# Paged attention whose every second sample reads latents stored turned

## The reference, cut to what matters

```python
past_c = cache_latent[j][page_table].reshape(bs, past_len, KV_LORA)      # 8 x 4096 x 256
past_r = cache_krope[j][page_table].reshape(bs, past_len, ROPE_DIM)      # 8 x 4096 x 64
past_k = cache_kscale[j][page_table].reshape(bs, past_len, MLA_HEADS)    # 8 x 4096 x 8
s = (jnp.einsum('bqhr,bkr->bhqk', ql, c) + jnp.einsum('bqhp,bkp->bhqk', qr, kr))
s = s * ks * SOFTMAX_SCALE
p = jax.nn.softmax(s, axis=-1)
o = jnp.einsum('bhqk,bkr->bqhr', p, c)
```

## Time and profile before

| | us |
|---|---|
| median of 3 runs | 3991.21 (3987.98 to 3994.84) |
| time of the profiled execution | 3988.52 |
| its span | 3986.4 |
| first gather of `mla_dec` starts | 2234.61 |
| last `back` of `mla_dec` starts | 2446.85 |
| issue of the first load of the stage behind it | 2465.32 |

### The profile page before, as it was taken

One profiled execution on the slowest core, in us unless ns is written; L12 is line 12 of the kernel. 1 busy time (PEld: TensorE's weight loads), 2 busy tenths in 40 slices (PEclk: granted clock), 3 DMA queues, 4 the chain that ended last, 5 costly groups with the idle time before them and its releaser, 6 DMA issues. The chain is left out here.

```text
span 3986.4 us, 45941 instructions
## 1 busy us (share of the span) xinstructions
PE 3005.8 (75%) x14557; PEld 1439.4 (36%) x14557; DVE 2474.6 (62%) x6084; ACT 1535.0 (39%) x4402; POOL 1289.7 (32%) x1172
## 2 busy tenths in 40 slices
PE   7997888777666677768757798776777876666666
PEld 6886775322212122223313575322232222222221
DVE  2665443676676667767773343476677677667675
ACT  2352121444343344446432221344544444334332
POOL 0004330444434333333441110233334344334433
PEclk9998788988778788888878898888888988787778
DMA  2211002999999999999996453799999999999998
GB/s 89 73 51 55 13 13 71 404 420 416 420 414 418 405 397 387 411 366 384 402 421 244 165 204 144 291 375 390 381 375 415 405 404 421 413 420 413 411 421 334
DMA packets 234350, 1261.33 MB, mean 316 GB/s; under 512 B 32008, under 2 KB 71952, under 8 KB 97552
## 3 DMA queue, kind: packets, MB, share of 16 engines
q0 software_dynamic: 153600, 1133.58, 69.8%
q1 hardware_dynamic: 80528, 125.08, 9.1%
HBM read 1244.25 MB, written 14.19 MB: 316 GB/s over the span
## 5 line engine op out<-in xcount | busy, mean ns | idle before, releaser
L1951 PE MATMUL acc<-ring,diag 128*64 128x512 f32 x4096 | 1339.0, 751 | 751.3 <-ACT diag L1650 748.9
L1569 POOL DMA_INDIRECT ring<-in_uv,idx x1024 | 1119.1, 1093 | 1895.3 <-PE acc L1951 1635.2
L1761 DVE SCALAR_TENSOR_TENSOR ring<-ring,rep 128x1024 f32<-128x1024 f32 x1024 | 1230.6, 1221 | 368.9 <-DMA ring<-in_uv,idx 309.3
L1951 PEld LDWEIGHTS acc<-ring,diag 128*64 128x64 f32 x4096 | 250.3, 158 | 1494.2 <-ACT diag L1650 1317.8
L1642 ACT ACTIVATE hg<-hs 128x1 f32<-128x1 f32 x1024 | 203.7, 199 | 1141.1 <-DVE ring L1761 1139.1
L1650 ACT ACTIVATE diag<-const,hgg 128x64 f32<-128x64 f32 x1024 | 356.4, 348 | 33.4
L1646 ACT ACTIVATE hgg<-hg,weigh_by 128x1 f32<-128x1 f32 x1024 | 302.0, 295 | 33.2
L1883 PE MATMUL big<-xnT,w 128*128 128x264 f32 (+1 forms) x960 | 297.1, 435 | 0.0
L1883 PEld LDWEIGHTS big<-xnT,w 128*128 128x128 f32 x960 | 174.8, 203 | 185.0 <-issue 166.4
L298 PE MATMUL acc<-xnT,w 128*128 128x260 f32 x1024 | 230.2, 386 | 0.7 <-ACT inp L419 0.7
L298 PEld LDWEIGHTS acc<-xnT,w 128*128 128x128 f32 x1024 | 196.3, 192 | 38.4 <-issue 7.5
(11 more groups left out here) (571 smaller groups left out, 4057.7 us busy)
## 6 DMA issues: line engine op xcount, KB each, us to landing
w<-in_w_peer SPq DMA_DIRECT2D x64, 512.0 KB
w<-in_w_gdn SPq DMA_DIRECT2D x32, 512.0 KB, 3.6
ring<-in_uv,idx POOLq DMA_INDIRECT x1024, 12.3
wo<-in_w_mla_out SPq DMA_DIRECT2D x8, 1024.0 KB, 11.5
wo<-in_w_uq SPq DMA_DIRECT2D x8, 768.0 KB, 14.2
out_ssm_s<-states SPq DMA_DIRECT2D x4, 1024.0 KB, 5.1
wo<-in_w_gdn_out SPq DMA_DIRECT2D x4, 1024.0 KB, 8.2
sk<-in_keys SPq DMA_DIRECT2D x64, 64.0 KB
```

The lines of the kernel that those rows point to most:

```text
L1569: pool.indirect_dma_start(out=ring[:, c % RING, :], out_offset=None, in_=uv, in_offset=bass.IndirectOffsetOnAxis(ap=idx[u % 2][:, c:c + 1] ...
L1761: dve.scalar_tensor_tensor(ring[:, c % RING, 0:D], ring[:, c % RING, 0:D], 1.0, rep[:, 2 * a + c // RING, :], ALU.mult, ALU.mult, accum_ou ...
L1951: last = pe.matmul(acc[i][rows(j), :], diag[:, r, :], ring[:, r, D + HALF * j:D + HALF * j + HALF], start=r == 0, stop=r == RING - 1)
```

## The change

Samples with `a` = 0 stay as they were. For samples with `a` = 1 a second copy of the cache, `cache_turned`, prepared on the host, holds each page with the channels as rows: 128 rows of 320 numbers (128 positions of channels 0 to 127, the same of channels 128 to 255, and the rotary channels of two positions one above the other). GpSimd gathers it page by page, 32 DMAs of 128 rows each, into the one buffer `turned`, and the scores of these samples read `turned` directly, in runs of 4 numbers with a distance of 320 between runs. Their `flips` and the three copies behind them are gone. The latents of these samples are still gathered in the old layout too, since `values` needs them; their `keys` gather is gone. `mla_qkv` also makes `pages.row`, the 256 row-number columns for the page gathers. GpSimd's loop is written out.

```diff
@@ mla_qkv
+                sp.dma_start(pages.lane[:, :], core.i["lane"]).then_inc(s["page"], 16)
+                sp.dma_start(pages.all[:, :], core.i["page_table"].rearrange("(o b) g -> o (b g)", o=1).to_broadcast([P, NS * PAGES])).then_inc(s["page"], 16)
...
-                dve.wait_ge(s["page"], 80)
+                dve.wait_ge(s["page"], 112)
+                dve.tensor_copy(pages.rowf[:, :], pages.all[:, :]).then_inc(s["gains"], 1)
+                dve.scalar_tensor_tensor(pages.rowf[:, :], pages.rowf[:, :], float(PAGE), pages.lane[:, 0:1].to_broadcast([P, NS * PAGES]), ALU.mult, ALU.add).then_inc(s["gains"], 1)
+                dve.tensor_copy(pages.row[:, :], pages.rowf[:, :])
@@ mla_dec, GpSimd
+                def pages_turned(v):
+                    for g in range(PAGES):
+                        pool.indirect_dma_start(out=turned[:, g, :], out_offset=None, in_=core.i["cache_turned"],
+                                                in_offset=bass.IndirectOffsetOnAxis(ap=pages.row[:, PAGES * v + g:PAGES * v + g + 1], axis=0)).then_inc(s["lt1"], 16)
...
-                for a in range(2):
-                    keys(a)
-                    latents(a)
-                    factors(a)
-                with pool.Fori(1, TURNS) as i:
-                    for a in range(2):
-                        apart(pool, at("idx", i - 1, a + 1), at("flip", i - 1, NG * (a + 1)))
-                        keys(a)
-                        apart(pool, at(f"soft{a}", i - 1, 1))
-                        factors(a)
-                        apart(pool, at("pv", i - 1, a + 1))
-                        latents(a)
+                keys()
+                latents(0)
+                factors(0)
+                pages_turned(1)
+                latents(1)
+                factors(1)
+                for i in range(1, TURNS):
+                    after(pool, at("idx", i - 1, 1), at("flip", i - 1, NG))
+                    keys()
+                    after(pool, at("soft0", i - 1, 1))
+                    factors(0)
+                    after(pool, at("pv", i - 1, 1))
+                    latents(0)
+                    after(pool, at("idx", i - 1, 2), at("dotted", i - 1, 2 * NG))
+                    pages_turned(2 * i + 1)
+                    after(pool, at("soft1", i - 1, 1))
+                    factors(1)
+                    after(pool, at("pv", i - 1, 2))
+                    latents(1)
@@ mla_dec, TensorE
+                def latent(a, g, e, j):
+                    if a == 0:
+                        return cT[g % 2][:, e, j, :]
+                    first = PAGE * e + GRP * (BQ * g + j)
+                    return turned[:, :, first:first + GRP]
...
-                    if n or not first:
-                        after(pe, at("half0", i, n - 1), at("half1", i, n - 1))
-                    flips(i, a, g)
+                    if a == 0:
+                        if g == 0:
+                            after(pe, (s["lc0"], i * 16 + 16), (s["lr0"], i * 16 + 16))
+                        if g == NG // 2:
+                            after(pe, (s["ld0"], i * 16 + 16))
+                        if g or not first:
+                            after(pe, at("half0", i, g - 1), at("half1", i, g - 1))
+                        flips(i, g)
                     if n or not first:
-                        after(pe, at("half0", i, n), at("half1", i, n), at("keyr", i, n), at("lined", i, n - 1))
+                        if a == 0 and g:
+                            after(pe, at("half0", i, g), at("half1", i, g), at("keyr", i, g))
+                        if a and g == 0:
+                            after(pe, at("half0", i, NG), at("half1", i, NG), at("keyr", i, NG))
+                        if a and g == 1:
+                            after(pe, at("lt1", i, 16 * PAGES))
+                        after(pe, at("lined", i, n - 1))
```

More of the change, by code:

```diff
@@ L2135, in mla_qkv @@
     with Marks(core, "qkv", gains=1, q_made=1, q_out=1, k_made=1, k_square=2, q_square=1, rope=4, stat=11,
-               root=2, q_done=2, page=80, wuk=16, number=2) as s, ExitStack() as ctx:
+               root=2, q_done=2, page=112, wuk=16, number=2) as s, ExitStack() as ctx:
         sq = core.sbuf(ctx, "sq", [P, H, QK])
@@ L2252, in __init__ @@
         self.idx = [core.sbuf(ctx, "idx", [P, 1], U32) for _ in range(2)]
+        self.all = core.sbuf(ctx, "all", [P, NS * PAGES], mybir.dt.int32)
+        self.lane = core.sbuf(ctx, "lane", [P, 1])
+        self.rowf = core.sbuf(ctx, "rowf", [P, NS * PAGES])
+        self.row = core.sbuf(ctx, "row", [P, NS * PAGES], U32)
 def mla_dec(core, q, ckvT, krTs, ksc, wuv, os, pages):
@@ L2275, in mla_dec @@
         c = [core.sbuf(ctx, "c", [P, PER, KL]) for _ in range(2)]
-        kr = [core.sbuf(ctx, "kr", [P, PER, RD]) for _ in range(2)]
+        kr = core.sbuf(ctx, "kr", [P, PER, RD])
+        turned = core.sbuf(ctx, "turned", [P, PAGES, TURNED])
         ks = [core.sbuf(ctx, "ks", [P, PER, H]) for _ in range(2)]
@@ L2396, in _, with flips, rope @@
                 pe.matmul(pO[:, :], core.ident, core.const[:, C_ID:C_ID + 2, :].rearrange("p a c -> p (a c)"), start=True, stop=True)
-                def flips(i, a, g):
+                def flips(i, g):
                     for j in range(BQ):
[L2401 to L2404, removed]
+                        pe.transpose(b0[g % 2][:, j, :], c[0][:, BQ * g + j, 0:P], core.ident)
+                        pe.transpose(b1[g % 2][:, j, :], c[0][:, BQ * g + j, P:], core.ident)
+                    if g or not isinstance(i, int):
+                        after(pe, at("keyr", i, g))
                     for j in range(BQ // 2):
-                        last = pe.transpose(b2[:, j, :], kr[a][:, BQ * g + 2 * j:BQ * g + 2 * j + 2, :].rearrange("p j r -> p (j r)"), core.ident)
+                        last = pe.transpose(b2[:, j, :], kr[:, BQ * g + 2 * j:BQ * g + 2 * j + 2, :].rearrange("p j r -> p (j r)"), core.ident)
                     last.then_inc(s["flip"], 1)
+                def latent(a, g, e, j):
[3 more added lines that the diff above has]
+                    return turned[:, :, first:first + GRP]
+                def rope(a, g, j):
+                    if a == 0:
+                        return rT[g % 2][:, j // 2, :]
+                    first = 2 * PAGE + GRP * ((BQ * g + j) // 2)
+                    return turned[:, :, first:first + GRP]
                 def scores(a, g):
@@ L2412, in scores @@
                         for j in range(BQ):
-                            pe.matmul(pL[COLS * j:COLS * j + COLS, :], ql[a][:, e, :], cT[g % 2][:, e, j, :], start=e == 0, stop=False)
+                            pe.matmul(pL[COLS * j:COLS * j + COLS, :], ql[a][:, e, :], latent(a, g, e, j), start=e == 0, stop=False)
                     for j in range(BQ):
-                        last = pe.matmul(pL[COLS * j:COLS * j + COLS, :], qr[a][:, j % 2, :], rT[g % 2][:, j // 2, :], start=False, stop=True)
+                        last = pe.matmul(pL[COLS * j:COLS * j + COLS, :], qr[a][:, j % 2, :], rope(a, g, j), start=False, stop=True)
                     last.then_inc(s["dotted"], 1)
@@ L2455, in values @@
                     after(pe, at("exped", i, 2 * a + 2), at("v_out", i, a))
+                    if a:
+                        after(pe, (s["lc1"], i * 16 + 16), (s["ld1"], i * 16 + 16))
                     for j in range(PER):
@@ L2718, in host @@
     w = np.asarray(x["gdn_w_in"])[0]
+    latent, rope = np.asarray(x["cache_latent"])[0], np.asarray(x["cache_krope"])[0]
+    turned = np.concatenate([
+        latent.reshape(-1, GRP, PER, 2, P).transpose(0, 4, 3, 2, 1).reshape(-1, P, 2 * PAGE),
+        rope.reshape(-1, GRP, PER // 2, 2, RD).transpose(0, 3, 4, 2, 1).reshape(-1, P, PAGE // 2)], 2).reshape(-1, TURNED)
     where = np.concatenate([np.arange(SEQ).reshape(NT, P), np.full((1, P), PAST)]).T.astype(np.float32)
```

35 lines of the change are left out of this document (20 added, 15 removed).

## The result

| | before | after |
|---|---|---|
| median, us | 3989.64 (3987.98 to 3994.84, 4 runs) | 4129.41 (4117.69 to 4141.07, 4 runs) |
| ratio, 95% interval | | 1.0348 (1.0317 to 1.0379) |
| span of the profiled execution | 3986.4 | 4115.9 |
| first gather of `mla_dec` to the first load of the stage behind it | 230.7 (2234.61 to 2465.32) | 374.3 (2225.44 to 2599.76) |
| one turn of two samples | 51.2 | 88.6, the next 90.1 |

The change costs 3.5%, where 1.5% was forecast, and 4129 lies far outside the range of 4027 to 4072. The stage became 143.6 us longer; what lies around it took 14 us less in this execution than in the one of before (9.2 of it ahead of the first gather), which is how the span grew by 129.5.

The account below looks back on a forecast made before the run. TensorE bounds `mla_dec` before; with the change a turn is a ring of 25.8 + 41.6 = 67.4 us against 51.2. The last `back` comes 56.9 us later, so 3988.5 becomes 4045.4, median 4048; range 4027 to 4072.

Parts of the forecast that it names:

- rest of the other sample's steps: In `mla_dec`, TensorE's 8 steps of the other sample, about 18 us, run during the page gathers and add nothing.
- first page gather to TensorE free to go on: In `mla_dec`, 32 page gathers issued, landed and TensorE woken: 38.6 + 2.8 + 0.2 = 41.6 us per turn.
- to the values: From the pages' landing to the first sample's values: scores at half clock, softmax chain, further scores, 8.0 us.
- to the next transposes: From the end of the values to the next sample's first transpose, as GpSimd gathers latents only behind the values: 9.2 us.
- last scores: Last scores of the `a` = 1 sample stand behind the next sample's step 0 transposes: 3.9 us at half clock.
- a gather by the piece: GpSimd gathers in a row start 1.244 us apart, 0.94 of it busy, whatever their bytes.
- the one buffer as a ring: `turned` exists once, so issuing page gathers cannot overlap with using them: each turn is gathering plus using, 67.4 us.
- the two terms for a low clock: After the pages land, clock taken as 0.50: 8.0 us to the values, 4.7 for values; 5.8 and 3.6 at full clock.
- Clock up: Rival: TensorE's clock stays or comes back at once; turn 62.4 us, +38, time 4029; chance 0.12.
- Dear gathers: Rival: GpSimd's page gathers cost 1.09 us busy each; +57 + 20 us, time 4068; chance 0.06.
- slow reads: Rival: TensorE reads `turned` slowly in the scores; +57 + 25 us, time 4073; chance 0.06.
- a GpSimd that keeps up: Rival: a page gather every 0.72 us or less, TensorE still sets the pace; time 3964; chance 0.04.

Follow-up runs that it names:

- e2: The changed kernel with page gathers of turns 1 to 3 fetching only 64 of 128 rows, leaving out part of the computation: 4130.02 us, ratio 1.0359.
- e7_fours: The changed kernel with a pause of 1.05 us on GpSimd behind every fourth page gather: 4092.65 us, ratio 1.026.
- e1: The kernel before, with 16 page gathers that nobody reads added on GpSimd behind each sample's latents: 4148.24 us, ratio 1.0405.
- e5: The kernel before, with sixteen GpSimd multiplications of 128x512 that nobody reads behind each sample's latents, no added gathers: 3988.95 us, ratio 1.0001.
- e4: The changed kernel with pages loaded by SyncE as plain DMAs, page numbers in registers, in place of GpSimd's gathers: 4031.84 us, ratio 1.0112.
- e3: The changed kernel with a pause on GpSimd (one product of 128x512) behind each page gather: 4200.7 us, ratio 1.0536.
- e6: The kernel before, with eight page gathers that nobody reads added on GpSimd behind each sample's latents: 4064.11 us, ratio 1.0189.

## Why the prediction was wrong

**The step that failed** is "TensorE has 8 steps of the other sample to do in it, about 18 + 4 us for values". The forecast put TensorE's work beside the row of gathers, since no semaphore of the program stands between them. In the profile TensorE got through some two more steps and then stood, since its signals to VectorE and ScalarE came up to 40 us late. The term "rest of the other sample's steps" was put at nothing on top of the row, and it measured 20.8 us. The turn, term by term from the rows above:

| term | forecast | measured |
|---|---|---|
| first page gather to TensorE free to go on | 41.6 | 45.2 (2320.35 to 2365.52) |
| the rest of the other sample's steps | 0, beside the row | 20.8 (to 2386.31) |
| to the values | 8.0 | 5.9 (to 2392.25) |
| values | 4.7 | 3.4 (next matmul at 2395.70) |
| to the next transposes | 9.2 | 8.9 (to 2404.59) |
| last scores | 3.9 | 4.4 (to 2408.96) |
| turn | 67.4 | 88.6 |

One term holds 20.8 of the 21.2 us. Over the whole stage: the first scores on `turned` come 72.1 us behind the first gather, forecast 46.4 (the 47.6 of the forecast's times less the 1.2 of `mla_qkv`), 25.7 more; the three turns up to the last sample's first scores take 268.7 us, forecast 202.2, 66.5 more; the rest to the last `back` 15.0, forecast 19.3, 4.3 less. That is 87.9 us, the whole difference of the two stages (374.3 measured, 230.7 + 56.9 - 1.2 forecast).

**Right were** a gather by the piece (1.25 us, 0.947 busy, bytes without effect, e2), the one buffer as a ring, the latents' wait behind the values (8.9), and the reads of `turned`: a matmul on it takes 273 ns in the median (512 of them), as one on `cT` does. There the Trainium skill's page "Advanced Engine Details and Errata", section "SBUF Cachelines", agrees with the trace. The ring's arithmetic is borne out where signals pass: e7_fours has 79.1, and without its 8.4 us of pauses that is 70.7 against 67.4.

**Mis-sized**, by 3.4 us in all, were the two terms for a low clock: TensorE had just worked for 20 us when it came to the pages, and its matmuls there take 0.27 us, the full clock's duration, where the forecast had the clock at 0.50. At the last scores the clock was down, as forecast (transposes of 0.42 us, 4.4 us against 3.9). The DMA engines were hidden, as forecast: from 2335 to 2359 they moved 133 GB/s at a share of 0.43, so the 5.2 MB of a sample's pages take 5.2 x 0.43 / 0.133 = 17 us of them, forecast 18. That the two agree is luck. The forecast had 4096 packets at 72 ns; the queue counts 48 a gather, 1536 for a sample, so a packet took some 175 ns.

**One more coincidence:** the two low-clock terms were 3.4 us too dear, and the first term, to TensorE free to go on, was 3.6 us too short, so the two errors cancel.

**The rivals.** "Clock up" had the two terms at the pages right (5.8 and 3.6, measured 5.9 and 3.4), had the last scores wrong (2.2, measured 4.4), and missed the cause. Dear gathers, slow reads and a GpSimd that keeps up are all refuted by the rows. The true case was not among them: a row of gathers that costs an engine which has nothing to do with it. The earlier trace rows could not show it. Its longest row is eight gathers at the very start, when TensorE had little to signal.

**What is shown and what is not.** Shown by taking away and adding: in this stage the loss needs gathers (e1, e5) issued by GpSimd (e4) back to back (e3, e7), and does not depend on half of their rows (e2) or on the ring (e1). Shown by the trace: TensorE's signals come late while VectorE's and ScalarE's are on time. Not told apart: whether it matters that GpSimd issues them or that they are indirect, since SyncE's loads in e4 are plain ones and no run has plain loads by GpSimd. And gathers in a row are not enough by themselves: in the PEER stages of the kernel before up to nine stand in a row (3275.13 to 3288.08, DMA share 0.99), and none of TensorE's signals in those stages is more than 0.03 us late. TensorE starts 46 matmuls in those 13 us, against 353 in 23 us of `mla_dec` (2314 to 2337); whether their number is what matters, no run tests. Why TensorE's signals are held is open. The Trainium skill's page "DMA: Bandwidth & Descriptors", section "SWDGE vs HWDGE vs iDMA", says that processors of GpSimd write the descriptors of its DMAs, and hardware those of SyncE's; e4 and e1 fall on the two sides of that line, but the page states no effect on TensorE, and no run here looks inside. That TensorE lacked instructions doesn't fit: the trace has two loads of instructions within the row (2321.39 and 2326.51, for whichever engine), 0.92 and 0.31 us long like those outside it, and signals are late while TensorE issues (2323.24 to 2328.95, and in e6). For the slow pace of its matmuls from 2326 to 2335 no run shows the reason.

## What to carry to other kernels

Before work is put "beside" a row of GpSimd gathers, look for a stretch of the profile in which that many stand back to back beside the same kind of work on TensorE (nine in a row beside few matmuls did no harm here), and see whether TensorE's consumers start on time there. If a row is needed, a pause of a microsecond behind every fourth gather let the signals through within 5 us here, and with loads by SyncE, the page number in a register, they were on time. And when one copy of a buffer makes a ring of loading and using, shorten the load's issue first and then see whether the DMA engines carry it: here loads by SyncE, a second queue and the later latents together only reached the old time.

## What the runs showed of the hardware that was not expected

- Back-to-back indirect gathers by GpSimd (1.25 us apart, 0.947 busy) beside `mla_dec`'s work delayed what TensorE signals by 2 to 6 us in a row's first 10 us, and by 40 us in a row of 32 (scores ended 2325.10, copied 2365.52); 8 gathers cost 9.2 us, 16 cost 19.4. Signals of VectorE were within 0.1 us throughout.
- Up to nine gathers in a row beside the PEER stages' fewer matmuls delayed no signal of TensorE by more than 0.03 us.
- A pause of 1.05 us behind every fourth gather was enough for TensorE to be busy 22.4 of 34 us within the row.
- During a row TensorE's own matmuls came one by one, 0.7 or 1.4 us apart.
- A gather of 64 rows of 1280 bytes took 903 ns and made 32 packets, one of 128 rows 947 ns and 48; a plain load of the same page by SyncE made 144.
- SyncE issued a load with a page number from a register every 0.83 us (12 in 10 us); ScalarE did so between its copies.
